# Sparse attention's causal mask and row maxima: mask products on TensorE, or a band added by VectorE

## The reference, cut to what matters

```
m_w = (kt <= t) & (kt > t - WINDOW) & (kt >= 0)
s_w = einsum(q, k_w) * scale;  p_w = masked_softmax(s_w, m_w);  o_w = p_w @ v_w
s_s, p_s, o_s: the same with the selected branch's keys and values
s_c = einsum(q, k_cmp) * scale; p_c = masked_softmax(s_c, cmp_end <= t); o_c = p_c @ v_cmp
o   = g0 * o_c + g1 * o_s + g2 * o_w
```

## Time and profile before

| | |
|---|---|
| median of 3 runs | 990.15 us (988.58 to 990.57) |
| span of the profiled execution, first to last instruction | 989.3 us |
| PE busy | 962.7 us, 97% of the span |
| PEld busy | 834.7 us, 84% |
| DVE, ACT, POOL busy | 473.2, 418.8, 443.0 us |
| mean granted TensorE clock | 0.989 |

### The profile page before, as it was taken

One profiled execution on the slowest core, in us unless ns is written; L12 is line 12 of the kernel. 1 busy time (PEld: TensorE's weight loads), 2 busy tenths in 40 slices (PEclk: granted clock), 3 DMA queues, 4 the chain that ended last, 5 costly groups with the idle time before them and its releaser, 6 DMA issues. The chain is left out here.

```text
span 989.3 us, 15834 instructions
## 1 busy us (share of the span) xinstructions
PE 962.7 (97%) x5910; PEld 834.7 (84%) x5910; DVE 473.2 (48%) x1363; ACT 418.8 (42%) x973; POOL 443.0 (45%) x588
## 2 busy tenths in 40 slices
PE   6999998999999999999999999999899999999798
PEld 6988888999999998888888878888688888888776
DVE  5231028777877774211210136678265556665411
ACT  5263236777777773312422333433323333223310
POOL 2443427878877852333443346668411111111131
PEclk9999999999999999999999999999899999999899
DMA  6332221111011012222722212223000000000031
GB/s 209 97 126 82 80 78 46 47 47 40 19 47 46 13 43 86 78 94 82 140 95 82 86 43 85 91 87 117 10 1 2 1 2 2 1 1 2 1 117 54
DMA packets 39253, 58.86 MB, mean 59 GB/s; under 512 B 8693, under 2 KB 22282, under 8 KB 39178
## 3 DMA queue, kind: packets, MB, share of 16 engines
q1 hardware_dynamic: 39136, 57.84, 18.6%
q10 hardware_dynamic: 42, 0.01, 0.0%
HBM read 55.62 MB, written 2.10 MB: 58 GB/s over the span
## 5 line engine op out<-in xcount | busy, mean ns | idle before, releaser
L94 PE MATMUL bank<-w_hi,h_hi 128*128 128x512 f32 (+2 forms) x480 | 187.9, 391 | 3.0 <-POOL w_lo L1284 1.9
L1356 POOL TENSOR_TENSOR w_lo<-w_raw,w_hi 128x2048 fp32r<-128x2048 f32 (+1 forms) x26 | 118.4, 4555 | 158.9 <-ACT w_hi L1131 158.9
L95 PE MATMUL bank<-w_lo,h_hi 128*128 128x512 f32 (+2 forms) x480 | 184.0, 383 | 0.0
L96 PE MATMUL bank<-w_hi,h_lo 128*128 128x512 f32 (+2 forms) x480 | 183.9, 383 | 0.0
L94 PEld LDWEIGHTS bank<-w_hi,h_hi 128*128 128x128 f32 x480 | 90.8, 189 | 21.3 <-issue 2.6
L96 PEld LDWEIGHTS bank<-w_hi,h_lo 128*128 128x128 f32 x480 | 90.8, 189 | 17.2
L95 PEld LDWEIGHTS bank<-w_lo,h_hi 128*128 128x128 f32 x480 | 90.9, 189 | 15.6
L1910 POOL TENSOR_TENSOR o_c<-o_c,o_sw 128x256 f32<-128x256 f32 x16 | 11.8, 736 | 184.7 <-DVE o_c L1976 184.7
L1131 ACT ACTIVATE w_hi<-w_raw 128x2048 fp32r<-128x2048 f32 (+1 forms) x26 | 49.2, 1891 | 78.9 <-PE bank L96 78.9
L1831 PE MATMUL bank<-kvr,probT 128*128 128x65 f32 x640 | 82.1, 276 | 0.0
L94 PE MATMUL bank<-w_hi,o_hi 128*128 128x512 f32 x192 | 77.5, 404 | 2.2 <-PEq L2005 2.2
(11 more groups left out here) (277 smaller groups left out, 2268.3 us busy)
## 6 DMA issues: line engine op xcount, KB each, us to landing
w_raw<-in_nsa_w_in SPq DMA_DIRECT2D x10, 1024.0 KB, 5.0
w_raw<-in_mla_w_in SPq DMA_DIRECT2D x8, 1024.0 KB, 5.1
w_raw<-in_mla_w_out SPq DMA_DIRECT2D x8, 1024.0 KB, 5.1
w_raw<-in_nsa_w_in SPq DMA_DIRECT2D x8, 984.0 KB, 5.0
w_raw<-in_mla_w_uq SPq DMA_DIRECT2D x8, 576.0 KB, 4.1
w_raw<-in_mla_w_ukv SPq DMA_DIRECT2D x16, 256.0 KB, 2.7
w_raw<-in_nsa_w_out SPq DMA_DIRECT2D x4, 1024.0 KB, 5.1
w_raw<-in_mla_w_in SPq DMA_DIRECT2D x4, 704.0 KB, 5.6
```

The lines of the kernel that those rows point to most:

```text
L94: nc.tensor.matmul(out, a[0], b[0], start=start, stop=False)
L95: nc.tensor.matmul(out, a[0], b[1], start=False, stop=False)
L96: return nc.tensor.matmul(out, a[1], b[0], start=False, stop=stop)
L1356: nc.gpsimd.tensor_tensor(w_lo[g % 2][:, :, 0:width], w_raw[g % 2][:, :, 0:width], w_hi[g % 2][:, :, 0:width].bitcast(F32), ALU.subtract). ...
```

## The change

First scores lose their mask products. VectorE's maximum becomes one instruction for each tile and branch: it adds a band (`band`, 384 columns of zeros and then `causal`) to the scores, writes the sum to a scratch tile in SBUF (`scored`, two of them), and returns the maximum over the columns, starting from −3e38. With no mask between, the two branches of tiles 0 and 1 become one product with a strided key operand. The maximum is no longer negated; ScalarE's copy of the row multiplies by −1. For the turned scores, one mask product serves both branches of blocks 2 and 3 (the identity is read twice, the output is strided); for units 0 to 3 it stays one a unit, but is issued behind both units' other products. `start` is then set only on the first branch's first product. `zeros` moves to a shared place and the `band` is built with one more memset on GpSimd.

```diff
+LEAST = -3e38
...
-        causal = keep("causal", [P, P], BF16)
+        band = keep("band", [P, SEQ], BF16)
+        causal = band[:, SEQ - P:SEQ]
...
-        zeros = keep("zeros", [P, NT * NC])
...
+                zeros = place("zeros", 82 * KB, [P, NT * NC])
...
-                    nc.gpsimd.affine_select(out=causal[:, :], in_=z, compare_op=ALU.is_ge, fill=NEG,
+                    nc.gpsimd.memset(band[:, 0:SEQ - P], 0.0)
+                    nc.gpsimd.affine_select(out=causal, in_=z, compare_op=ALU.is_ge, fill=NEG,
...
-                negmax = at_slab("negmax1", 58.5, [P, 2, NT, 2])
+                rowmax = at_slab("rowmax1", 58.5, [P, 2, NT, 2])
+                scored = [at_slab(f"scored{a}", 60 + 2 * a, [P, SEQ]) for a in range(2)]
...
-                        for w, b in enumerate(branches):
-                            dst = first_bank[k % 2][:, w * keys:(w + 1) * keys]
-                            nc.tensor.matmul(dst, qT_hi[a][0:DK, tok], kT_hi[0:DK, b, n // HPG, 0:keys],
-                                             start=True, stop=False)
-                            last = nc.tensor.matmul(dst[:, tok], identb[:, :], causal[:, :], start=False, stop=True)
-                        last.then_inc(f_done, 1)
+                        b0, nb = branches[0], len(branches)
+                        nc.tensor.matmul(first_bank[k % 2][:, 0:nb * keys].rearrange("p (b c) -> p b c", b=nb),
+                                         qT_hi[a][0:DK, tok], kT_hi[0:DK, b0:b0 + nb, n // HPG, 0:keys],
+                                         start=True, stop=True).then_inc(f_done, 1)
...
-                        nc.tensor.matmul(dst, kT_hi[0:DK, b, g, keys], qT_lo[a][:, j * P:], start=True, stop=False)
+                        nc.tensor.matmul(dst, kT_hi[0:DK, b, g, keys], qT_lo[a][:, j * P:], start=w == 0, stop=False)
...
-                        return nc.tensor.matmul(dst[:, 0:P], causal[:, :], identb[:, :], start=False, stop=True)
+
+                    def mask(n, u):
+
+                        j, branches = block_of[u]
+                        nb, left = len(branches), left_of(j)
+                        dst = score_bank[(U * n + u) % 3][:, 0:nb * left].rearrange("p (b c) -> p b c", b=nb)[:, :, 0:P]
+                        nc.tensor.matmul(dst, causal, identb[:, :].unsqueeze(1).to_broadcast([P, nb, P]), start=False,
+                                         stop=True).then_inc(s_done, 1)
...
-                            large_term(n, u, 0, u).then_inc(s_done, 1)
+                            large_term(n, u, 0, u)
+                        for u in range(2):
+                            mask(n, u)
...
                         scores(n, 2)
                         scores(n, 3)
+                        mask(n, 2)
+                        mask(n, 3)
                         values(n, 0)
                         scores(n, 4)
+                        mask(n, 4)
...
                         scores(n, 5)
+                        mask(n, 5)
...
-                        nc.scalar.activation(qT_hi[n % 2][DK:DK + 2, :], x_bank[0:2, :], ACT.Copy).then_inc(m_in, 1)
+                        nc.scalar.activation(qT_hi[n % 2][DK:DK + 2, :], x_bank[0:2, :], ACT.Copy,
+                                             scale=-1.0).then_inc(m_in, 1)
...
-                        b0, nb = branches[0], len(branches)
-                        nc.vector.tensor_reduce(negmax[:, n % 2, i, b0:b0 + nb],
-                                                first_bank[k % 2][:, 0:nb * keys].rearrange("p (b c) -> p b c", b=nb),
-                                                AX.X, ALU.max, negate=True).then_inc(max_done, 1)
+                        if k >= 2:
+                            dve.wait_ge(max_done, k - 1)
+                        for w, b in enumerate(branches):
+                            last = nc.vector.tensor_tensor_reduce(
+                                scored[k % 2][:, w * keys:(w + 1) * keys], first_bank[k % 2][:, w * keys:(w + 1) * keys],
+                                band[:, SEQ - keys:SEQ], 1.0, LEAST, ALU.add, ALU.max, rowmax[:, n % 2, i, b:b + 1])
+                        last.then_inc(max_done, 1)
```

More of the change, by code:

```diff
@@ L371, in trunk @@
         slab_at = nc.sbuf_base
-        keep("slab", [P, 136 * KB // 4 + 192])
+        keep("slab", [P, 136 * KB // 4 + 144])
         at_slab = lambda name, kb, shape, dt=F32: nc.alloc_sbuf_tensor_at(name, shape, dt, offset=slab_at + int(kb * KB))
@@ L765, in scores @@
                         nc.tensor.matmul(dst, hi[:, 1, tok], lo[:, 2, keys], start=False, stop=False)
-                        nc.tensor.matmul(score_bank[i % 2][:, tok], identb[:, :], causal[:, :], start=False,
+                        nc.tensor.matmul(score_bank[i % 2][:, tok], identb[:, :], causal, start=False,
                                          stop=True).then_inc(s_done, 1)
@@ L1752, in turn_max @@
                         for i in range(NT):
-                            last = nc.tensor.transpose(x_bank[0:2, i * P:(i + 1) * P], negmax[:, n % 2, i, :],
+                            last = nc.tensor.transpose(x_bank[0:2, i * P:(i + 1) * P], rowmax[:, n % 2, i, :],
                                                        ident[:, :])
@@ L1780, in scores @@
                             small_terms(n, u, w, b)
-                            last = large_term(n, u, w, b)
-                        last.then_inc(s_done, 1)
+                            large_term(n, u, w, b)
                     def start_scores(n):
```

## The result

The changed kernel takes 976.76 us in the median of 4 runs (975.47 to 980.91), the kernel before in the same comparison 990.36. The ratio is 0.9868, with a 95% interval of 0.9850 to 0.9886: 13.1 us faster by the ratio (the two medians lie 13.6 apart), more than twice the forecast 5.4, and outside the stated range of 978.5 to 992.5 at its low end.

A forecast was written before the change was run, and what follows sets the result against it. PE and a loop through VectorE and PE were taken to bind together; legs −0.69 and +0.37 gave −0.32 a head, −4.8 over fifteen periods, −5.4 with the ends: 984.8 us, forecast 981.5 to 988, whole range 978.5 to 992.5.

The forecast's parts named there:

- The loop and what it does: Second layer's attention: each head's period is VectorE's leg (5.75 us) plus PE's leg (7.90) in series, 13.65, falling to 13.33.
- VectorE's leg +0.37: Four fused maxima in VectorE's leg lengthen it by 0.37 us a head, mostly through a second instruction reading the maximum out.
- Rival 1: The maximum comes out for nothing: VectorE's leg grows only 0.04 us, time 979.8, or 979.0 with cheap mask pair; 27%.
- PE's leg −0.69: From turned maxima to next compressed scores, PE saves 0.69 us a head (0.61 to 0.75) by fewer masks and joined products.
- Mask behind mask: Scores 0/1 and 2/3: a mask beside another costs 0.08 us (bounds 0.05 and 0.12), saving 0.09 for both.
- The shared mask of 256 columns: In scores 4 and 5, one wider mask for both branches was taken as 0.09 us.
- PE's whole relief 1.09: PE's saving per head: 0.69 us in its leg plus 0.40 beside VectorE's leg; 17.4 us if PE alone bound.
- PE and this loop bind together: Before the change, PE's work beside VectorE's leg is as long as that leg, to within 0.1 us.
- GpSimd's memset, the exponentials, the sign on the copy: Extra memset hidden; exponentials 0 and 2 released 0.2 to 0.4 us later, absorbed; ScalarE's copy keeps its 0.58 us.
- The two ends of the stage: Attention stage's ends: the lead-in before head 0 gains 0.3 us, the last head 0.26.
- Rivals 2, 4 and 5: Serial read of the maximum, 996.6 us (9%); fused instruction at half rate, 1007 (3%); clock falls, 1008 (4%).
- Rival 3: In between: additions near 0.16 us each, or PE waits for an exponential behind moved masks; within 2 us of before; 9%.

The follow-up runs named there:

- e4: The changed kernel with a one-column copy on VectorE behind each fused instruction; median 979.95 us, period 13.01.
- e5: The changed kernel with VectorE's output scaling of tiles 0 to 2 moved behind maxima 4 and 5; median 970.49 us, period 12.28.
- e7: e5 with the one-column VectorE copies of e4 added; median 969.50 us, period 12.26.
- e6: The kernel before with VectorE's output scaling of tiles 0 to 2 moved behind maxima 4 and 5; median 991.90 us, period 13.65.
- e1: The kernel before with only the turned scores' masks changed; first scores keep their masks and the reductions stay; median 985.80 us, period 13.30.
- e2: The changed kernel with the turned scores' masks put back as before; first scores stay without masks, with fused maxima; median 982.96 us, period 13.12.
- e8: The changed kernel with the masks of units 0 to 3 back between the units' products, shared masks kept; median 980.80 us, period 12.92.

## Why the prediction was wrong

**The loop and what it does: right.** The period was to be VectorE's leg plus PE's leg after the change. That sum by itself proves nothing, since two legs that meet at the turning add up to the period whatever binds. e4 shows that a longer leg of VectorE lengthens the period one for one; e5 and e7 show where this stops. PE's load was to idle for 0.7 to 0.9 us before turning the maxima; it was 0.75. This agreement is luck: PE itself was to lose 13.33 − 12.56 = 0.77 a head, and it lost 12.77 − 12.28 = 0.49. The load's wait is longer than PE's loss because the load can start ahead of its product: by 0.21 us in e6, where it waits for nothing, and by nothing in the changed kernel.

**VectorE's leg +0.37: wrong, and the largest miss.** This is the step "Taken over, maxima 2, 3 and 4 cost 0.01 + 0.09 more each", with 0.07 for the last. Measured: 0.06 in all four together, near the lower bound of 0.04. At the turning nothing of it shows, since the forecast counted its 5.75 up to the turning, and 0.06 of that was slack before PE. The second instruction exists, as the Trainium skill's page "VectorE: DVE Perf Modes", section "Two Vector instructions with no wait between them", says; the trace agrees. But it starts together with the next main one and ends with the main one's tail (0.08 us, 799.96 to 800.04, where the main one ends at 800.03). I priced it by ScalarE's row, where the read does shift the next instruction by 0.09. An instruction on the same engine of one column would have been nearer and still wrong: e4's copy costs 0.07. Nothing in the trace of before showed the price. Rival 1, with 27%, had the cost nearly right, and its 979.8 (979.0 with a cheap mask pair) was off by the misses on PE's side. 0.37 × 15 = 5.6 us, 0.31 of the 0.37 by the read's price and 0.06 by the slack.

**PE's leg −0.69: too small by 0.19.** By parts, each read in the profile after and confirmed by e1, e2 and e8:
- Mask behind mask: 0.07, and the mask's own distance to what follows is 0.06, no more than a mask had before. With the large terms at 0.24 each, scores 0/1 save 0.07 and scores 2/3 0.08, in place of 0.09 for both (+0.06; e8).
- The shared mask of 256 columns: 0.04, not 0.09 (twice, +0.08 with rounding).
- The short product behind a 512-column product: 0.06, not 0.11 (+0.05).

Together 0.19 × 15 = 2.9 us. The sum of the two misses, 8.5, is what lay between the forecast of 984.8 and the measured 976.8 but for half a microsecond.

**PE's whole relief 1.09: too small.** PE's own course in e5 is 12.28, so the relief is 1.37. The same cheap product behind a long one comes after first scores 2/3 and 4/5 as well: first scores 4/5 went from 0.75 to 797.99 − 797.43 = 0.56, as forecast, but the first value product behind them costs 0.06 in place of 0.11, and so does the one behind 2/3. With the 0.19 of PE's leg, that is the 0.28.

**"PE and this loop bind together": half right.** They were level to within 0.06, but it was PE that set 13.65; e6 shows that the loop could be shortened for nothing. It spoiled the number only by those 0.06 of slack, since the loop binds as soon as PE is relieved by more. It hid rather how the change could be completed: the freed time was handed to a wait.

**GpSimd's memset, the exponentials, the sign on the copy: right.** The copy still lasts 0.58 us. The memset lasts 0.42, and GpSimd then idles 15.40 until its next work, at 18.22.

**The two ends of the stage: near in the sum, wrong in the parts.** The lead-in got 0.43 us shorter (0.3 forecast) and the last head 0.03, where 0.26 was forecast; what holds the last head was not traced. With these, the first period's 0.25 and 14 × 0.88, the stage's 13.07 is accounted for to 0.04.

Rivals 2, 4 and 5 fall by the profile: the read isn't serial, 512 columns take 684 ns, and the clock is 1.00 from 726 to 908 though PE waits in each head; one window of it stands below. Rival 3 falls too, with additions of some 0.01 each and by e8, and rival 6 by PE's wait and e4.

```profile
768.00:782.00 14.00, 13.67 (x109) 12.32 (x108) 8.97 (x40) 4.86 (x11) 2.19 (x3) 1.00 0.01 2
```

## What to carry to other kernels

When two engines feed each other once per iteration, write down both the loop (one leg per engine) and each engine's own course. Measure a leg to the end of the engine's own work, and the gap from there to the other engine's start beside it: that gap tells which of the two binds, and how much slack there is. An edit that relieves the fuller engine moves the bound to the loop, and then a step in the other engine's leg that nobody waits for soon is worth moving behind the handover, as e5 did for another 6 us; the same move was worth nothing before. A mask as a product cost more here than its own row shows: 0.04 us itself and up to 0.09 in the product behind it, so it pays to share masks, or to put them side by side.

## What the runs showed of the hardware

- VectorE's read of the accumulator (83 ns) runs beside the next main instruction. Two fused instructions of 512 columns start 0.61 apart, two reductions 0.60. A one-column copy lasts 0.15 us and adds 0.07.
- A fused add and maximum over 512 float columns of PSUM and a bf16 band takes 684 ns, the plain reduction 680.
- The next product starts 0.06 us after a 128-column one that stands right behind a 512-column one, and 0.11 after one in a stream of short ones. A mask of 256 columns costs the same 0.04 as one of 128.
- TensorE's granted clock stayed at 1.00, its level of 2.4 GHz, from 726 to 908 us, with PE some 0.5 us a head of 12.8 behind its own course (0.34 of it marked as idle in the profile).
